# Two up tiles formed together behind a norm, a third place for split weights, and the last activation between accumulations

## What is computed

```python
# end of first_block
mix = jnp.concatenate([y_ssd, y_rwkv], axis=-1) @ w_out[l]
h = h + _rms_norm(mix, post_mix_norm[l])
hn = _rms_norm(h, pre_ffn_norm[l])
u = _causal_dwconv(hn @ ffn_w_up[l], ffn_conv_w[l], ffn_conv_b[l])   # 3 taps along the tokens
gate, val = jnp.split(u, 2, axis=-1)
f = (jax.nn.silu(gate) * val) @ ffn_w_down[l]                        # 2816 hidden channels
h = h + _rms_norm(f, post_ffn_norm[l])
...
# start of second_block
h = rms_norm(x, g_norm1[l]) * (1.0 + sc1) + sh1
proj = h @ w_in                                                      # hybrid_mixer
```

## Time and profile before

| what | value |
|---|---|
| median of three runs | 1792.78 us (1789.63, 1801.59, 1792.78) |
| the profiled execution | 1786.85 us, of which the span of its records is 1785.0 us |
| granted clock of PE, mean | 0.98 |
| PE busy | 1678.0 us, 94% of the span |
| DVE busy | 1202.3 us, 67% |
| POOL busy | 676.7 us, 38% |
| ACT busy | 481.5 us, 27% |

### The profile page before, as it was taken

The page is one execution under the profiler, slowest core; times in us unless marked ns, Lnnn a source line. Parts: engine busy times, 40 slices in busy tenths (PEclk is TensorE's granted clock), DMA queues, the critical chain, the costliest instruction groups (busy, mean ns, idle before and its releaser), DMA issues.

```text
span 1785.0 us, 29266 instructions
## 1 busy us (share of the span) xinstructions
PE 1678.0 (94%) x11954; PEld 1299.6 (73%) x11954; DVE 1202.3 (67%) x1601; ACT 481.5 (27%) x739; POOL 676.7 (38%) x382
## 2 busy tenths in 40 slices
PE   7999988899699999999699999999998997999998
PEld 6887667777487777777478788778777866666665
DVE  6959786656588888888675179387554616666674
ACT  4122344422210011001231122221231005545452
POOL 4665000023166666666346534336344641000000
PEclk9999999999899999999899999999999998999999
DMA  6222531131242222222222212113212245788884
GB/s 246 95 94 95 178 108 50 51 120 49 77 172 95 94 94 94 79 88 91 94 72 95 95 48 72 48 48 115 88 51 71 94 189 201 293 353 328 342 336 161
DMA packets 34069, 230.52 MB, mean 129 GB/s; under 512 B 4132, under 2 KB 4388, under 8 KB 8232
## 3 DMA queue, kind: packets, MB, share of 16 engines
q1 hardware_dynamic: 30240, 214.48, 33.1%
q10 hardware_dynamic: 2136, 10.24, 1.5%
q0 software_dynamic: 1584, 4.21, 0.7%
HBM read 220.98 MB, written 9.50 MB: 129 GB/s over the span
## 4 chain that ended last, share of the span: by engine, by line
PE 80%; DVE 12%; ACT 3%; DMA 3%; issue 2%; DVEq 0%; POOL 0%; SPq 0%; POOLq 0%; ACTq 0%
PE psum L421 79%; DVE arena L1715 3%; DVE arena L1709 2%; DMA arena<-units 2%; PE psum L425 2%; ACT arena L1305 1%; DVE arena L1712 1%; DVE expert_lo L1709 1%; DMA normed<-units 1%; ACT expert_hi L1305 1%; DVE residual L1709 0%; DVE arena L2344 0%; DVE smalls L2341 0%; DVE tiny L1723 0%; DVE yb_lo L1709 0%
## 5 line engine op out<-in xcount | busy, mean ns | idle before, releaser
L1305 ACT ACTIVATE arena<-psum 128x512 f32<-128x512 f32 (+3 forms) x298 | 150.7, 521 | 816.4 <-PE psum L421 751.7
L421 PE MATMUL psum<-arena 64*64 64x64 f32 (+6 forms) x2852 | 218.8, 261 | 24.3 <-DVE arena L1709 12.8
L421 PE MATMUL psum<-normed_hi,w_in_hi 128*128 128x512 f32 x504 | 202.5, 402 | 7.4 <-DVE in_lo L1709 4.8
L421 PEld LDWEIGHTS psum<-arena 64*64 64x64 f32 (+4 forms) x2852 | 147.5, 146 | 80.4 <-issue 48.7
L421 PE MATMUL psum<-normed_hi,w_in_lo 128*128 128x512 f32 x504 | 200.6, 398 | 0.0
L421 PE MATMUL psum<-in_lo,w_in_hi 128*128 128x512 f32 x504 | 199.0, 395 | 0.0
L1715 DVE SCALAR_TENSOR_TENSOR arena<-arena,fixed_data 128x512 f32<-128x512 f32 x138 | 184.6, 1339 | 13.5 <-DVE arena L1712 0.2
L1709 DVE TENSOR_TENSOR arena<-arena,psum 128x512 f32<-128x512 f32 (+2 forms) x200 | 110.5, 588 | 110.4 <-PE psum L421 64.5
L2591 POOL TENSOR_TENSOR w_ff_lo<-weight_ring,w_ff_hi 128x1024 fp32r<-128x1024 f32 x66 | 167.1, 2532 | 5.5
L2591 POOL TENSOR_TENSOR w_in_lo<-weight_ring,w_in_hi 128x1024 fp32r<-128x1024 f32 x63 | 159.2, 2528 | 5.2
L2589 POOL TENSOR_SCALAR w_in_hi<-weight_ring 128x1024 fp32r<-128x1024 f32 x63 | 72.4, 1149 | 203.6 <-PE psum L421 192.9
(11 more groups left out here) (251 smaller groups left out, 3426.9 us busy)
## 6 DMA issues: line engine op xcount, KB each, us to landing
weight_ring<-units SPq DMA_DIRECT2D x124, 1024.0 KB, 4.9
arena<-units SPq DMA_DIRECT2D x55, 1024.0 KB, 7.6
normed<-units SPq DMA_DIRECT2D x20, 1024.0 KB, 7.9
slots<-arena ACTq DMA_DIRECT2D x7, 516.0 KB, 8.8
arena<-slots SPq DMA_DIRECT2D x7, 516.0 KB, 5.7
fixed_data<-fixed ACTq DMA_DIRECT2D x1, 2944.0 KB, 9.6
arena<-x SPq DMA_DIRECT2D x4, 512.0 KB, 5.9
arena<-bias_rows ACTq DMA_DIRECT2D x2, 896.0 KB, 4.4
```

The source lines that it names most:

```text
L421: return nc.tensor.matmul(o, l, r, start=start, stop=stop)
L1305: return nc.scalar.activation(o, i, func, **kw)
```

## The change

- PE forms the first two up tiles together: for each part k it makes three matmuls for the one tile and three for the other (`pair_of_tiles`). The same holds for the first two tiles of `p2`; there `forget` comes one tile later.
- The second sums of each pair of norms go to bank 0.
- The first chunk of w_ff and of w_in2 has a place of its own (`WeightsAfter`). POOL splits it before it waits for the end of the product ahead, and splits the third chunk once all eight residual tiles are updated, without waiting for `split_used`.
- On DVE the loop is a round shorter; the last round is written out, and in it `finish_gate` comes between the first four accumulations and the last four.

```diff
+        class WeightsAfter(Weights):
+            def __init__(self, name, off, chunk, hi_off, lo_off):
+                super().__init__(name, off)
+                self.chunk = chunk
+                self.first = [part(name + n, o, CHUNK) for n, o in (("_first_hi", hi_off), ("_first_lo", lo_off))]
+            def slot(self, q):
+                if q == self.chunk:
+                    hi, lo = self.first
+                    return hi[:, :], lo[:, :]
+                return super().slot(q)
...
-        w_ff = Weights("w_ff", F_W)
+        q_ff = 2 * 14 + KT
+        q_in2 = q_ff + 6 * NF
+        w_ff = WeightsAfter("w_ff", F_W, q_ff, 8208, 13344)
-        w_in2 = Weights("w_in2", n_arena - 8192)
+        w_in2 = WeightsAfter("w_in2", n_arena - 8192, q_in2, 16896, 18432)
...
+            def pair_of_tiles(weights, rhs, outs, ready):
+                w = [[part_.rearrange("p (k c) -> p k c", k=KT) for part_ in take(weights)] for _ in range(2)]
+                o = [open_(what, k, b) for what, k, b in outs]
+                for k in range(KT):
+                    pe.wait_ge(sem(ready), k + 1)
+                    for i, (hi, lo) in enumerate(w):
+                        begun = mm(o[i], hi[:, k, :], rhs.hi(k), k == 0, False)
+                        if k == i * (KT - 1):
+                            begun.then_inc(sem("split_used"), 1)
+                        mm(o[i], lo[:, k, :], rhs.hi(k), False, False)
+                        last = mm(o[i], hi[:, k, :], rhs.lo(k), False, k == KT - 1)
+                        if k == KT - 1:
+                            close(last, *outs[i][:2])
...
-            sums("sum_pre_ffn", sq8, "sq_pre_ffn")
+            sums("sum_pre_ffn", sq8, "sq_pre_ffn", 0)
...
-                for i in range(4):
+                if ready:
+                    pair_of_tiles(w_ff, in_ff, [(kind + "_up", (phase, sub, i), i) for i in range(2)], ready)
+                for i in range(2 if ready else 0, 4):
...
-            sums("sum_1", sq8b, "sq_1")
+            sums("sum_1", sq8b, "sq_1", 0)
...
-            project("p2", 1, w_in2, in2, MISC, ready="h_ready")
-            emptied(pe, "p2", MISC)
-            for m in range(2):
-                close(mm(open_("forget", m, 4 + m), M("gate2")[:, m * P:(m + 1) * P], p2(MISC)), "forget", m)
-            project("p2", 4, w_in2, in2)
+            pair_of_tiles(w_in2, in2, [("p2", MISC + i, i) for i in range(2)], "h_ready")
+            for t in range(8):
+                w = take(w_in2)
+                close(tile_of(w, KT, P, 0, in2, open_("p2", t, t % 4), True), "p2", t)
+                if t == 0:
+                    emptied(pe, "p2", MISC)
+                    for m in range(2):
+                        close(mm(open_("forget", m, 4 + m), M("gate2")[:, m * P:(m + 1) * P], p2(MISC)), "forget", m)
...
-            with dve.Fori(0, times) as it:
+            with dve.Fori(0, times - 1) as it:
...
+            it = times - 1
+            conv_gate((it, 1), "loop", 1, it)
+            accumulate("ffn", "loop", 0, it)
+            finish_gate((it, 1), 1)
+            conv_gate((it, 2), "loop", 0, it)
+            accumulate("ffn", "loop", 1, it, range(4))
+            finish_gate((it, 2), 0)
+            accumulate("ffn", "loop", 1, it, range(4, KT))
             accumulate("ffn", "last", 0)
...
-                    if i:
+                    if i > 1 or i == 1 and (c or weights not in (w_ff, w_in2)):
                         pool.wait_ge(sem("split_used"), q + c if it is None else it * 4 + (q + c))
...
+            def split_after(weights, n, what, k, n_updated):
+                split_unit(weights, 0, None, 1)
+                filled(pool, what, k)
+                split_unit(weights, 0, None, 2, 1)
+                unit[0] += 2
+                pool.wait_ge(sem("x_updated"), n_updated)
+                split_unit(weights, 1, None, 1, 0)
+                split_unit(weights, 1, None, 2, 1)
+                split_rest(weights, 2, n)
...
-            filled(pool, "mix", KT - 1)
-            split_units(w_ff, 3 * NF, 2)
-            filled(pool, "ffn_down", ("last", 0, KT - 1))
-            split_units(w_in2, 18, 2)
+            split_after(w_ff, 3 * NF, "mix", KT - 1, KT)
+            split_after(w_in2, 18, "ffn_down", ("last", 0, KT - 1), 2 * KT)
```

More of the change, by code:

```diff
@@ L909, in _, with sums @@
                 mix(t, range(4 if t == 2 else 0, KT), 4 if t == 2 else 0)
-            def sums(what, names, ready):
-                token_sums(what, names, lambda k: (sem(ready), k + 1))
+            def sums(what, names, ready, b=4):
+                token_sums(what, names, lambda k: (sem(ready), k + 1), b)
             sq8 = [A(SQ1 + k * T) for k in range(KT)]
@@ L927, in up @@
                     o = open_(kind + "_up", k, i, it, 2)
-                    close(tile_of(w, KT, P, 0, in_ff, o, True, None if i else ready), kind + "_up", k)
+                    close(tile_of(w, KT, P, 0, in_ff, o, True), kind + "_up", k)
             def down(kind, phase, j, it=None):
@@ L2133, in finish_gate, with accumulate @@
                     split(acts, 2 * sub + i, "ffn_act_ready")
-            def accumulate(kind, phase, sub, it=None):
-                for m in range(KT):
+            def accumulate(kind, phase, sub, it=None, tiles=range(KT)):
+                for m in tiles:
                     k = (phase, sub, m)
@@ L2153, in _ @@
                 finish_gate((it, 2), 0)
-            ch.leave(times)
+            ch.leave(times - 1)
+            it = times - 1
[6 more added lines that the diff above has]
+            accumulate("ffn", "loop", 1, it, range(4, KT))
             accumulate("ffn", "last", 0)
@@ L2574, in unit_loaded, with split_unit @@
                 pool.wait_ge(sem(f"weights{u % RING}_loaded"), v if it is None else it * (16 * per // RING) + v)
-            def split_unit(weights, i, it=None, halves=2):
+            def split_unit(weights, i, it=None, halves=2, first=0):
                 u, q = unit[0] + i, chunk[0] + 2 * i
                 unit_loaded(u, it, 2)
-                for c in range(halves):
-                    if i:
+                for c in range(first, halves):
+                    if i > 1 or i == 1 and (c or weights not in (w_ff, w_in2)):
                         pool.wait_ge(sem("split_used"), q + c if it is None else it * 4 + (q + c))
@@ L2591, in split_unit, with split_units, split_rest @@
                     nc.gpsimd.tensor_tensor(lo, raw, hi.bitcast(F32), ALU.subtract).then_inc(sem("split_ready"), 1)
-            def split_units(weights, n, between=0, last=2):
+            def split_units(weights, n, last=2):
                 split_unit(weights, 0)
-                unit[0] += between
-                times = (n - 1) // 2
+                split_rest(weights, 1, n, last)
+            def split_rest(weights, begun, n, last=2):
+                times = (n - begun) // 2
                 with pool.Fori(0, times) as it:
                     ch.enter(it, 4)
-                    split_unit(weights, 1, it)
-                    split_unit(weights, 2, it)
+                    split_unit(weights, begun, it)
+                    split_unit(weights, begun + 1, it)
                 ch.leave(times)
-                if n % 2 == 0:
+                if (n - begun) % 2:
                     split_unit(weights, n - 1, None, last)
```

## The result

The changed kernel takes 1780.15 us (median of 20 runs, 1773.36 to 1795.96) against 1792.73 us of the kernel before (20 runs, 1788.55 to 1805.02): ratio 0.9927, interval 0.9906 to 0.9949, or about 13 us. Measured once more, beside experiments, the ratio was 0.9958, 0.9932 to 0.9984, or 7.5 us. The forecast was 10.0 us less, 1781.2.

What follows compares the result with a forecast made beforehand. PE carries 80% of the chain, DVE 12%, so gains come where PE waits. Terms 3.6 + 2.8 + 3.6 = 10.0 us, taken from the executions' middle of 1791.2, give 1781.2 us; range 1773.6 to 1790.

Steps and rivals of the forecast that it cites:

- three parts: Norms ahead of the up projection 3.6 us, last activation of the loop 2.8, norms ahead of p2 3.6.
- The addition: First residual addition of each norm stage, freed of GpSimd's second split: 0.8 us ahead of up, 0.6 ahead of p2.
- The sums: Second norms' sums in bank 0, made while squares come in, only the last following: 1.2 us earlier per norm.
- The pair and the clock: First two up tiles interleaved: starts 2.0 us earlier, ends 4.6 earlier; 3.6 taken because the clock may fall.
- low stretch: Seven matmuls at the lower clock level inside the two interleaved tiles, each costing 0.205 us more, 1.5 us together.
- The last activation: End of the loop: activation after four accumulations, PE restarts 1.6 us earlier, clock 1.2 more; 2.8 us, 1.6 to 4.1.
- the collision: Last activation's cast meets POOL's low-part split, 2.50 us in place of 0.43; without it the gain is 6.5 us.
- What is late next: VectorE's taps of tiles 0 to 2 take 11.8 us, up to 506.8, holding the first norms' gain within 0.7.
- VectorE taking the gain: Rival, 0.14: each of tiles 0 to 2 meets a split; first norms gain only 0.8 us, total 7.2, 1784 us.
- two collisions: Rival, 0.07: POOL's high part also delays the last activation, which gains 0.5 us; total 7.7, 1783.5 us.
- no pair: Rival, 0.05: a late second chunk or bank makes PE run tile after tile; total 6.6 us, 1784.6.
- The clock through whole pairs: Rival, 0.04: low clock throughout both interleaved pairs costs 9.9 us each; kernel 8 us slower, 1799.

Runs made afterwards that it cites:

- late split: Changed kernel with the first weight chunk split behind the product's end again, together with the second chunk; ratio 0.9960 to the kernel before.
- bank 4: Changed kernel with the second norms' sums back in PSUM bank 4, behind the multiplication that frees it; ratio 0.9963 to the kernel before.
- third place at end: Changed kernel plus an extra place for the first chunk of the last split unit, so GpSimd splits it without waiting for TensorE; ratio 0.9951 to the kernel before.
- without the hold: Changed kernel minus GpSimd's wait, before splitting the third chunk, until VectorE has done the residual additions; ratio 0.9980 to the kernel before.
- tile after tile: Changed kernel with the two interleaved tiles undone: the first takes the parts one by one, the second follows; ratio 0.9958 to the kernel before.
- extra matmuls: Changed kernel plus unread matmuls behind each of the second norms' sums, two behind the last; ratio 0.9957 to the kernel before.
- matmuls up to the pair: Changed kernel plus a place for the last unit's first chunk, unread matmuls behind the second norms' sums and three more behind their last rows; ratio 0.9922 to the kernel before.

## Why the prediction was right

**The sum held, and so did its three parts.** Predicted 3.6, 2.8 and 3.6; measured 3.70, 2.92 and 3.59 in the first profile, and the same within 0.01 in the second.

**The addition:** 0.8 and 0.6 predicted; 0.80 and 0.66 by the late split.

**The sums:** 1.2 predicted, 1.1 and 1.4 by bank 4. That only one square's sums are left behind the last square is as it was said, at 0.66 us each.

**The pair and the clock** came out right in sum by two errors that cancel. The prediction let the pair gain all of TensorE's waiting, 4.6 us, and took off 1.0 for a low stretch inside it, part of the 1.5 that such a stretch would cost. In the changed kernel's two profiles no pair had such a stretch. The lower level lay earlier, on the spreading of the root: 2.08 us in place of 1.16, in every norm with the sums spread out and nothing in their rests. So the first up matmul came 0.98 us earlier, not 2.0, and the pair gained 2.7 us, not 1.6. The prediction never asked what the sums' new order does to the clock behind them; it was luck that these 0.9 us are about the 1.0 that it had taken off in another place. Where a pair did catch a low stretch, in 6 of 20, it cost 1.5 to 1.9 us: the size was right, its frequency was not.

Taken one by one, the steps add up in the first norms: 0.80 for the addition, 1.1 for the sums and 2.7 for the pair, less 0.9 on the spreading, make 3.7, and the stage gained 3.70. So theory B, by which single steps are worth little, does not hold. Ahead of p2 they make 3.9 (0.66, 1.4, 2.76, less 0.92) against 3.59; that difference was not followed up.

**The last activation:** the order was as said, four accumulations, activation, then the others, with the cast beside the split: 2.52 us, as the row of 2.50 from the first pass had it. The restart gained 1.94 us, predicted 1.6; the clock gave most of the remaining 1.0, where 1.2 was allowed, since 8 matmuls are still slow. Free of the collision 6.5 was forecast, and "third place at end" brought 5.93.

The Trainium skill ("SBUF — State Buffer", section "Who interferes with whom") lets issue order decide between VectorE and GpSimd and the loser wait for the whole instruction. The runs agree in three places: the cast, 2.52 against 0.43; the residual addition, 1.47 against 0.68; the two additions without the hold, 2.78 against 1.28. The prediction put it for two SBUF inputs and named the cast as its row, which has one; the additions have two. The price here is the difference between 2.9 and 5.9 us in the last activation, half of it the lower clock behind the longer rest.

**What is late next.** VectorE made the taps of tiles 0 to 2 of the first pass in 11.7 us, up to 507.06 (11.8 forecast), and then met tile 3:

```profile
505.52 1.54 DVE L1751 SCALAR_TENSOR_TENSOR arena<-arena,fixed_data 128x512 f32<-128x512 f32 x2
507.22 0.55 DVE L1748 TENSOR_SCALAR arena<-arena,fixed_data 128x512 f32<-128x512 f32 x1 [0.15 <-ACT arena L1341]
507.80 2.19 DVE L1751 SCALAR_TENSOR_TENSOR arena<-arena,fixed_data 128x512 f32<-128x512 f32 x2
```

It waited 0.15 us for ScalarE's copy at 507.22, so VectorE did not take the gain; from the third up tile to the last matmul of the loop's end both kernels need the same time within 0.3 us (356.46 and 356.24). Behind the forget products VectorE's idle time is 27.55 us in place of 33.04: it covered the tile by which they come later.

**The rivals.** VectorE taking the gain, two collisions and no pair did not happen. The clock through whole pairs did not either: the worst pair lost 1.9 us where 9.9 were feared. The order of the tiles did not decide the level: tile after tile began low in the first norms and high ahead of p2, as the pairs did in two kernels.

What stays open: what decides in an execution whether the lower level ends ahead of the pair or inside it. The same code ran both ways, and no edit here removed it for certain: with extra matmuls one pair of 6 had a low stretch, without them 5 of 14.

## What to carry to other kernels

Price an edit that starts work earlier for what it does to TensorE's use, too: matmuls handed out one by one as inputs arrive may be done sooner and leave the next steps at half the clock. Interleave two tiles over the parts of an input that arrives slowly; it needs one more place for weights and no other engine. And where a copy of weights is made by GpSimd beside VectorE's chain, move the copy, by a place or by a wait, into a stretch where VectorE reads PSUM or rests: here three such moves were worth 0.7 to 3 us each.

## What had not been expected of the hardware

The clock was at the lower level in all 14 spreadings that followed spread-out sums. It had fallen ahead of the first sum in three of them and during the sums in eleven, and was not back by the spreading in any. The sums came in groups of eight matmuls, most of them of 0.43 to 0.66 us; TensorE's rests were no longer than 0.9 us between groups (2.1 once a norm in the kernel without the hold), up to 1.9 us ahead of the first and 1.7 to 1.8 us ahead of the spreading. With small matmuls in the rests the spreading had the higher level in 6 of 6; during the sums themselves the clock could still be low, until 478.9 in the kernel with the matmuls up to the pair.

Behind a rest of 2.4 us at the last activation the clock was low for 7 or 8 matmuls in six profiles and for none in a seventh, in the same code.
